# A decoder block in split float32 on one core: the order of the three products of a tile, and the layout of the second feed-forward network's input

## What is computed

```python
def swiglu(h, w_gate, w_up, w_down):
    return (jax.nn.silu(h @ w_gate) * (h @ w_up)) @ w_down

hs = hs + 0.5 * swiglu(rmsnorm(hs, ffn1_norm), ffn1_w_gate, ffn1_w_up, ffn1_w_down)   # 2048 -> 5632 -> 2048
hs = hs + token_mixing(rmsnorm(hs, mix_norm), w_in, b_in, ..., w_out)                 # 2048 -> 5120, 2048 -> 2048
hs = hs + 0.5 * swiglu(rmsnorm(hs, ffn2_norm), ffn2_w_gate, ffn2_w_up, ffn2_w_down)
out = rmsnorm(hs, final_norm)[:, 16:]
```

## Time and profile before

| | |
|---|---|
| runs | 1882.8, 1873.69, 1882.98 us; median 1882.8 |
| profiled execution, its own time | 1873.64 us |
| its span, first to last instruction | 1871.8 us |
| TensorE, matmuls busy | 1859.9 us (99%), 13017 recorded |
| TensorE, weight loads busy (beside the matmuls) | 1758.7 us (94%) |
| VectorE busy | 1112.3 us (59%) |
| ScalarE busy | 922.3 us (49%) |
| GpSimd busy | 5.9 us (0%) |
| DMA | 342.26 MB, 183 GB/s over the span |

### The profile page before, as it was taken

How to read it: one execution, slowest core, us unless ns; L and a number is a source line. 1 busy time by engine, 2 the same in 40 slices (tenths; PEclk the granted TensorE clock), 3 DMA queues, 4 the chain that set the end, 5 groups by cost and what they waited for, 6 DMA issues and landing times.

```text
span 1871.8 us, 32101 instructions
## 1 busy us (share of the span) xinstructions
PE 1859.9 (99%) x13017; PEld 1758.7 (94%) x13017; DVE 1112.3 (59%) x1218; ACT 922.3 (49%) x1173; POOL 5.9 (0%) x17
## 2 busy tenths in 40 slices
PE   9999999999999999999999999999999999999998
PEld 9999999999999999999999999888888888888886
DVE  7555555555554545468899887555566655544444
ACT  6434333343343444359888665444444444443443
POOL 1000000000000000000000000000000000000000
PEclk9999999999999999999999999999999999999999
DMA  6655555555555555555666566666656666666664
GB/s 222 192 178 173 175 178 170 178 174 173 179 172 178 176 175 178 176 174 170 187 185 178 173 201 186 189 189 189 190 179 188 191 192 193 210 193 190 193 190 134
DMA packets 283357, 342.26 MB, mean 183 GB/s; under 512 B 10639, under 2 KB 223985, under 8 KB 283152
## 3 DMA queue, kind: packets, MB, share of 16 engines
q1 hardware_dynamic: 282672, 340.44, 58.6%
q10 hardware_dynamic: 320, 0.53, 0.1%
q0 software_dynamic: 288, 0.19, 0.0%
HBM read 339.02 MB, written 2.10 MB: 182 GB/s over the span
## 4 chain that ended last, share of the span: by engine, by line
PE 98%; DVE 1%; DMA 0%; ACT 0%; SPq 0%; issue 0%; DVEq 0%
PE ps L466 20%; PE ps L467 20%; PE ps L468 20%; PE ps L473 17%; PE ps L474 9%; PE ps L568 4%; PE ps L567 4%; PE ps L569 4%; DMA x_tok<-in_x 0%; DVE w_lo L886 0%; PE ps L428 0%; PE ps L585 0%; DVE zc L1098 0%; PE ps L591 0%; DVE ln_mu L912 0%; SPq L323 0%
## 5 line engine op out<-in xcount | busy, mean ns | idle before, releaser
L886 DVE TENSOR_TENSOR w_lo<-raw,w_hi 128x1024 fp32r<-128x1024 f32 x639 | 781.7, 1224 | 652.5 <-ACT w_hi L650 647.4
L650 ACT ACTIVATE w_hi<-raw 128x1024 fp32r<-128x1024 f32 x639 | 675.5, 1058 | 845.6 <-PE ps L468 505.6
L466 PE MATMUL ps<-x_hi,w_hi 128*128 128x272 f32 (+2 forms) x2048 | 588.1, 287 | 1.2 <-DVE x_lo L895 1.2
L467 PE MATMUL ps<-x_lo,w_hi 128*128 128x272 f32 (+2 forms) x2048 | 587.3, 287 | 0.0
L468 PE MATMUL ps<-x_hi,w_lo 128*128 128x272 f32 (+2 forms) x2048 | 583.4, 285 | 0.0
L473 PE MATMUL ps<-x_both,w_hi 128*128 128x512 f32 x1408 | 488.4, 391 | 0.0
L474 PE MATMUL ps<-x_both,w_lo 128*128 128x256 f32 x1408 | 394.1, 280 | 0.0
L467 PEld LDWEIGHTS ps<-x_lo,w_hi 128*128 128x128 f32 x2048 | 386.4, 189 | 0.1
L466 PEld LDWEIGHTS ps<-x_hi,w_hi 128*128 128x128 f32 x2048 | 384.5, 188 | 1.5 <-DVE w_lo L1120 1.4
L468 PEld LDWEIGHTS ps<-x_hi,w_lo 128*128 128x128 f32 x2048 | 385.4, 188 | 0.0
L473 PEld LDWEIGHTS ps<-x_both,w_hi 128*128 128x128 f32 x1408 | 263.3, 187 | 57.8
(11 more groups left out here) (148 smaller groups left out, 1146.5 us busy)
## 6 DMA issues: line engine op xcount, KB each, us to landing
raw<-in_ffn_w_up SPq DMA_DIRECT2D x176, 512.0 KB, 3.6
raw<-in_ffn_w_down SPq DMA_DIRECT2D x176, 512.0 KB, 4.6
raw<-in_ffn_w_gate SPq DMA_DIRECT2D x175, 512.0 KB, 3.7
raw<-in_w_in SPq DMA_DIRECT2D x80, 512.0 KB, 3.5
raw<-in_w_out SPq DMA_DIRECT2D x32, 512.0 KB, 4.7
x_tok<-in_x SPq DMA_DIRECT2D x4, 512.0 KB, 7.9
gain_tok<-in_final_norm SPq DMA_DIRECT2D x1, 1024.0 KB, 5.3
out_y<-o_tok SPq DMA_DIRECT2D x2, 512.0 KB, 2.9
```

The lines of the kernel that those rows point to most:

```text
L466: pe.matmul(dst, w_high, act_high, start=first, stop=False)
L467: pe.matmul(dst, w_high, act_low, start=False, stop=False)
L650: act.activation(w_hi[s][:, :], raw[s][:, :], ACT.Copy).then_inc(hi_ready, 1)
L886: dve.tensor_tensor(w_lo[s][:, :], raw[s][:, :], w_hi[s][:, :].bitcast(F32), ALU.subtract).then_inc(lo_ready, 1)
```

## The change

In `product` the low activations move first: high weights by low, high by high, low by high. The number of matmuls, weight loads and columns is the same. `x2_both` is laid out [128, 2, 16, 256]: all high slices, and 16384 bytes further all low slices. The 512 columns of L473 are now two runs of 1024 bytes, and the slices of neighbouring k lie 1024 bytes apart and not 2048. The writers and readers of `x2_both` are indexed to match. Nothing else is changed, `down2` neither.

```diff
-        x2_both = at("x2_both", x_at, [P, KD, 2, SEQ], F32R)
+        x2_both = at("x2_both", x_at, [P, 2, KD, SEQ], F32R)
...
                 dst = ps[:, bank, 0:n]
-                pe.matmul(dst, w_high, act_high, start=first, stop=False)
-                pe.matmul(dst, w_high, act_low, start=False, stop=False)
+                pe.matmul(dst, w_high, act_low, start=first, stop=False)
+                pe.matmul(dst, w_high, act_high, start=False, stop=False)
                 return pe.matmul(dst, w_low, act_high, start=False, stop=last)
...
                                     m = wide_product(bank, w_hi[s][:, cols], w_lo[s][:, cols],
-                                                     x2_both[:, k, :, :], x2_both[:, k, 0, :],
+                                                     x2_both[:, :, k, :], x2_both[:, 0, k, :],
                                                      k == 0, k == KD - 1)
...
-                dst = x2_both[:, t, 0, :] if phase == "gu2" else x_hi[:, t, toks]
+                dst = x2_both[:, 0, t, :] if phase == "gu2" else x_hi[:, t, toks]
...
-                high, low_part = ((x2_both[:, t, b, :] if phase == "gu2" else (x_hi, x_lo)[b][:, t, toks])
+                high, low_part = ((x2_both[:, b, t, :] if phase == "gu2" else (x_hi, x_lo)[b][:, t, toks])
                                   for b in (0, 1))
```

## The result

| | before | changed |
|---|---|---|
| median of 20 runs | 1873.72 us | 1878.52 us |
| lowest, highest | 1873.29, 1882.98 | 1878.08, 1887.81 |
| runs at the lower value | 12 of 20 | 11 of 20 |
| profiled execution, span | 1871.8 us | 1876.6 us |

The ratio is 1.0031, with a 95% interval of 1.0017 to 1.0045: slower by 4.8 us. It lies inside "within 0.5%", which had most of my chance, but the forecast said that nothing moves, and something did. Both kernels fall on two values 9.3 us apart, 8 and 9 runs of 20 on the upper one.

What follows compares the result with a forecast made beforehand. TensorE's back-to-back matmul steps were taken to bound the kernel. The terms summed 0 + 0 + 0 = 0 against the profiled 1873.6 us; the forecast was 1880.0 us because runs fall on two values, with a range of 1855 to 1898.

Steps and rivals of the forecast that it cites:

- within 0.5%: Whole kernel: time within 0.5% of the kernel before, the jump alone included; chance 0.6.
- TensorE bounds the kernel: Whole kernel: TensorE's matmuls fill 99% of the span, nothing feeds it late, so only the matmul steps can change the time.
- I take 0 ns for the reordering: Order in product, 9024 steps: no change; bounds 15.0 us faster (3008 repeats saving 5 ns) to 16.9 us slower.
- the opening group's repeats: gu1's opening group: 22 steps, some repeating a slice, average 124.5 ns against 125.0 in the steady part, so repeats cost nothing.
- differ by only 0.3 ns: Mean steps of gu1 and down1, whose slices follow differently, are this close; argued against the faster rival.
- The formula cited beside it: Warm matmul step is N / 2.4 + 2.5 ns, by columns alone: order worth nothing, though it gives 115.8 of gu1's 125.0.
- The slower rival: Product stages up to out_cf: repeating a slice raises overhead to 13.3 ns, 16.9 us slower, 24.2 with gu2's jump; chance 0.2.
- The faster rival: Product and gu2: cheap repeats (120 not 125 ns) or better alignment, 18.4 us less, 1855.2 us; chance 0.2.
- up to 1905: The slower rival's time on the upper of the two run values; 1890.5 us, up to 1898, on the profiled one.
- Layout, writers and reader: x2_both: writers 0 us; gu2's 1408 two-run wide matmuls 0 us, bounds 7.3 us slower to 3.4 us faster.
- First matmul: Kernel's first matmul now reads x_lo, for which it already waited 1.2 us: 0 us.
- The two values: Whole kernel: runs fall at 1873.7 or 1882.8 and 1883.0 us, 9.2 apart; forecast 1880.0, nearer the value seen twice.

Runs made afterwards that it cites:

- e3: Changed order (low, high, high) with the gaps between high and low x and a tensors taken out: 1881.48 us, gu1 536.3, down1 266.0.
- e4: Order before (high, low, high) with the gaps between high and low x and a tensors taken out: 1881.49 us, gu1 536.3, down1 266.0.
- e17: Changed kernel with only the gap between a_hi and a_lo set to 64 bytes instead of 128: median 1876.62 us, down1 263.4.
- e2: Kernel before with the two-region x2_both layout alone, order as before: 1873.51 us, ratio 0.9993; its profiled execution took 1882.96 us.
- e14: Order before with 128 bytes between x_hi and x_lo instead of 64, a gap as before: gu1 534.0 us, down1 263.4, ag 96.46.
- e7: Kernel before with product as high by high, low weights by high, high weights by low: gu1 536.3 us, down1 263.7.
- e8: Kernel before with product as low weights by high, high by high, high by low: gu1 536.3 us, down1 263.7.
- e5: Kernel before, order kept, with y_lo moved 64 bytes further: 1882.74 us; out_sc and out_cf together 92.4 us.
- e13: Changed kernel with 128 bytes between x_hi and x_lo and 64 between a_hi and a_lo: gu1 534.0 us, down1 263.4.
- e10: Order before, x2_both in two regions, the low one alone begun 64 bytes further: gu2 488.65 us.
- e15: e10 again, timed: median 1873.66 us of 12 runs, ratio 0.9998; 3 runs at 1878.1 to 1878.3 us.
- e9: Order before, x2_both in two regions, both begun 64 bytes further: gu2 491.8 us.
- e16: e14 again, timed: median 1876.9 us; 11 of 12 runs between 1876.6 and 1877.4 us, one at 1875.16.

## Why the prediction was wrong

- **TensorE bounds the kernel, and only the steps can change the time:** right. All 4.8 us are in the steps, none in a wait.
- **"I take 0 ns for the reordering":** this is the step that failed. It measured 4.8 us over the 9024 steps, 0.53 ns each, inside the bounds (15.0 faster to 16.9 slower), so the mechanism that I left at nought was of the right place and a small size. I took the opening group's repeats for proof. They were read at 10 ns a row, and the mean of 22 steps, 124.5 ns, can't show half a nanosecond. They also stand in the one group of gu1 that the change leaves alone: the opening group takes 27.55 to 27.61 us in all 19 traces, whatever the order and the gaps, where a later group grew by 0.11. I had also written that gu1 and down1 "differ by only 0.3 ns" and drawn from it that the overhead doesn't hang on the order; 0.5 ns was the whole effect. The formula cited beside it from the Trainium skill ("TensorE: Matmul & The Clock Gate", back-to-back issue gap) gave no support either: that section states it for an isolated matmul, and has the spacing in a stream of weight loads and matmuls, such as this one, set by both.
- **The slower rival, "repeating a slice is dear":** right in sign, wrong in cause. With a repeat in every product the orders tie without gaps (e3, e4), and e17 takes down1's loss away with the repeats still there. In gu1 the changed order stays at least 2.2 us behind the best of the old one at every gap that was tried. No stage went to 13.3 ns on top; in the changed kernel gu1 and down1 reached 12.2 (125.6 - 113.3, unrounded).
- **The faster rival's argument,** that the alignment could fall better, named what counts, though with a saving of 5 ns a repeat that nothing here showed. It fell worse, since the gaps fit the old order. (The slower rival's "up to 1905" is too low by its own terms: 1882.8 + 24.2 is 1907.)
- **Layout, writers and reader, 0 us:** right. The two runs in one matmul cost nothing that shows (488.6 us in both, e2 1873.51 against 1873.52), so the penalty for a new line of which the Trainium skill ("SBUF — State Buffer", specifications) speaks is not seen here for one jump in 512 columns. **First matmul:** right, the wait is 1.2 us again.
- **The two values:** I forecast 1880.0 because I couldn't tell which value a median falls on. It fell on the lower one in both kernels.

## What to carry to other kernels

When an engine is busy 99% of the time and its steps are longer than its streaming, compare stages by counts in long stretches: half a nanosecond a step shows there and in no single row. Where tensors carry odd gaps, an order and its gaps are one choice, and a new order has to be tried with gaps of its own before it is judged: that gave back down1's loss here, and not gu1's. If runs of one program fall on two values, profile both before averaging them: here one stage in another rhythm was worth twice the change.

## What the runs showed of the hardware

- The length of a 272-column stage depends on the order of the slices together with the places where they begin. gu1 took 531.8, 534.0 to 534.1 or 536.3 us and nothing else, in 19 traces, and in gu1 kernels with the same jumps took the same. But the jumps don't fix a length by themselves (ag and gu1 in e14). The weights' sequence had no effect (e7, e8).
- The three lengths lie in equal steps: a group of gu1 after the opening takes 24.00, 24.11 or 24.21 us, so each of its 16 cycles of twelve matmuls (four k, three products) is 6.7 ns longer from one to the next. Why, and where in the engine it arises, was not tried.
- gu2 has two rhythms with `x2_both` on a multiple of 512 bytes, 346.7 and 353.3 ns a pair, 6.7 ns apart as well, and one program can have either. It can change at L488, even within one execution (e5, e13), and from there on holds for the rest of the stage. Whether this difference and gu1's have one cause is not shown. With the low slices shifted 64 bytes a third one of 350.0 ns showed ahead of L488 (e10, e15), and a run time 4.6 us up in 3 of 12; with both shifted it was 348.9 ns behind L488 (e9).
- At 256 columns, where each next k begins at the same place modulo 256 (out_sc and out_cf), none of the four forms of the product and neither of the two places of `y_lo` changed 92.4 us by 0.1.
- Some runs of the kernel before and of e2 lay at 1871.8 to 1872.1 us, 1.6 us below the common value, and one of e16 lay 1.7 us below its own. None of them was profiled, and which stage it is stays open.
